# Values of 64-wide heads stationary in column halves, outputs split straight from PSUM, probabilities scaled on GpSimd

## What is computed

```python
s = jnp.einsum('bqhd,bkhd->bhqk', q_i, k_i).astype(jnp.float32) + bias[None]
s = jnp.where(valid[None, None, None, :], s, NEG_INF)
p = jax.nn.softmax(s, axis=-1).astype(v.dtype)
return jnp.einsum('bhqk,bkhd->bqhd', p, v_i)
```

## Time and profile before

| | us |
|---|---|
| median of 3 runs | 2388.64 (2388.24 to 2388.89) |
| the profiled execution | 2387.63 |
| its span, first to last instruction | 2385.8 |
| PE busy | 2359.8 |
| DVE, ACT, POOL busy | 1457.3, 1213.2, 139.7 |

### The profile page before, as it was taken

One profiled execution on the slowest core, in us unless ns is written; L12 is line 12 of the kernel. 1 busy time (PEld: TensorE's weight loads), 2 busy tenths in 40 slices (PEclk: granted clock), 3 DMA queues, 4 the chain that ended last, 5 costly groups with the idle time before them and its releaser, 6 DMA issues.

```text
span 2385.8 us, 30340 instructions
## 1 busy us (share of the span) xinstructions
PE 2359.8 (99%) x11608; PEld 1975.4 (83%) x11608; DVE 1457.3 (61%) x2224; ACT 1213.2 (51%) x1838; POOL 139.7 (6%) x133
## 2 busy tenths in 40 slices
PE   8999999999999999999999999999999999999999
PEld 7888878878888888788888888888888889888887
DVE  5556775565557855565487656654755577556554
ACT  5555544435556444354466654544544476555443
POOL 1430000014210000000000000000000000000000
PEclk9999999999999999999999999999999999999999
DMA  8545456545455565555554445655555544445553
GB/s 299 167 152 198 163 202 234 185 160 170 159 190 168 179 221 184 169 186 193 170 191 145 159 142 168 208 184 180 203 190 190 176 160 142 159 155 190 177 194 106
DMA packets 118078, 427.55 MB, mean 179 GB/s; under 512 B 13616, under 2 KB 14384, under 8 KB 116912
## 3 DMA queue, kind: packets, MB, share of 16 engines
q1 hardware_dynamic: 117792, 425.56, 52.9%
q10 hardware_dynamic: 144, 0.07, 0.0%
HBM read 424.52 MB, written 1.05 MB: 178 GB/s over the span
## 4 chain that ended last, share of the span: by engine, by line
PE 95%; DVE 3%; ACT 1%; DMA 1%; issue 0%; POOL 0%; DVEq 0%; ACTq 0%
PE bank L1878 28%; PE bank L1880 27%; PE bank L1879 27%; PE bank L1935 5%; PE bank L1866 1%; PE bank L1867 1%; PE bank L1868 1%; DVE wl L1446 0%; PE bank L1980 0%; DMA raw<-in_weights 0%; PE bank L1953 0%; PE bank L2003 0%; ACT wh L1235 0%; DVE x L1611 0%; DVE xl L1458 0%
## 5 line engine op out<-in xcount | busy, mean ns | idle before, releaser
L1235 ACT ACTIVATE wh<-raw 128x1024 fp32r<-128x1024 f32 (+1 forms) x778 | 814.9, 1052 | 916.0 <-PE bank L1880 876.7
L1446 DVE TENSOR_TENSOR wl<-raw,wh 128x1024 fp32r<-128x1024 f32 (+1 forms) x778 | 939.3, 1222 | 462.1 <-ACT wh L1235 457.9
L1878 PE MATMUL bank<-wh,xh 128*128 128x512 f32 (+1 forms) x2176 | 867.2, 399 | 9.3 <-DVE xl L1458 6.1
L1880 PE MATMUL bank<-wh,xl 128*128 128x512 f32 (+1 forms) x2176 | 848.6, 390 | 0.0
L1879 PE MATMUL bank<-wl,xh 128*128 128x512 f32 (+1 forms) x2176 | 846.7, 389 | 0.0
L1878 PEld LDWEIGHTS bank<-wh,xh 128*128 128x128 f32 x2176 | 410.4, 189 | 91.8 <-issue 12.5
L1880 PEld LDWEIGHTS bank<-wh,xl 128*128 128x128 f32 x2176 | 410.0, 188 | 86.3
L1879 PEld LDWEIGHTS bank<-wl,xh 128*128 128x128 f32 x2176 | 411.0, 189 | 78.1
L1878 PE MATMUL bank<-wh,act_h 128*128 128x512 f32 x528 | 207.1, 392 | 0.0
L1880 PE MATMUL bank<-wh,act_l 128*128 128x512 f32 x528 | 205.6, 389 | 0.0
L1879 PE MATMUL bank<-wl,act_h 128*128 128x512 f32 x528 | 205.5, 389 | 0.0
(11 more groups left out here) (339 smaller groups left out, 2233.9 us busy)
## 6 DMA issues: line engine op xcount, KB each, us to landing
raw<-in_weights SPq DMA_DIRECT2D x760, 512.0 KB, 3.3
raw<-in_weights SPq DMA_DIRECT2D x16, 384.0 KB, 3.0
ln<-in_ln SPq DMA_DIRECT2D x4, 1024.0 KB, 6.4
bias<-in_bias SPq DMA_DIRECT2D x2, 1024.0 KB, 10.5
b_merge<-in_b_merge SPq DMA_DIRECT2D x2, 1024.0 KB, 5.6
gain<-in_gain_ffn SPq DMA_DIRECT2D x4, 512.0 KB, 3.8
decay<-in_decay SPq DMA_DIRECT2D x2, 768.0 KB, 12.0
x<-in_x SPq DMA_DIRECT2D x2, 512.0 KB, 5.1
```

The source lines that it names most:

```text
L1235: act.activation(wh[:, u % NH, 0:used(u)], raw[:, u % NR, 0:used(u)], ACT.Copy).then_inc(hi_done, 1)
L1446: dve.tensor_tensor(wl[:, u % NR, 0:used(u)], raw[:, u % NR, 0:used(u)], wh[:, u % NH, 0:used(u)].bitcast(F32), ALU.subtract).then_inc(lo_ ...
L1878: pe.matmul(out, h, w_h, start=st.first and i == 0, stop=False)
L1880: last = pe.matmul(out, lo, w_h, start=False, stop=st.last and i == st.nk - 1)
```

## The change

Values and probabilities change sides. Of each pair of heads the values (64 columns wide) are stationary, head h in column half 0 to 63 of the array and head h+1 in 64 to 127, and the transposed probabilities are the moving side: 256 columns for the first key tile, 128 for the second. `OB` then holds the outputs already transposed, features on the partitions, and a new step `o_split`, once every four heads, splits it straight into the high and low parts: ACT copies, DVE subtracts. `ca_out`, `aa_out` and the transposes of the outputs go. Since queries now lie along the columns, the probabilities are scaled before their transpose: a new step `even` takes the reciprocals of the sums on DVE, and POOL multiplies `Pn` by them, four multiplies a pair; `probs_T` waits for POOL (`evened`) in place of ACT (`soft`). A function `heads` lays out both attentions: in round j the evening of pair j-1, the scores of pair j, the values of pair j-2, then the two transposes of pair j-1. The exponential of the sink term is taken for every pair. `m_spread` moves ahead of the attention, and buffers of `ob` and `ha` move.

The strings of the weave are new, for all side work. In block 1 eight dense units (those of `rq` and `rk`) now stand ahead of the first turn of `cq`, where there was one, and seven in place of one behind the last turn. In dense units behind the start of the weave, the first side steps of block 1 then stand so: turns of `cq` at 8, of `ck` at 10, the scores of pair 0 at 11 and of pair 1 at 12 (with the evening of pair 0 ahead of it), transposes of head 0 at 13 and head 1 at 14, scores of pair 2, values of pair 0 and transpose of head 2 at 15. In the two blocks together the number of units is unchanged.

```diff
-UNITS_AMONG_1 = "10122203110102121111010010110201111101011111111111223210111011101011421"
-UNITS_AMONG_2 = "00030102010110200201000111002010210020020100011300000100100411111101000101021021011"
-LAG = 2
+UNITS_AMONG_1 = "802011011100011000011101113201120100110103021301223110011010102011207"
+UNITS_AMONG_2 = "0001020110011121010210100200101111001110050010111011110011101101000101020040102"
...
+def heads(p, of, n, scores, kept):
+
+
+    turn, done = {}, {}
+    for j in range(n + 2):
+        if 1 <= j <= n:
+            i = 2 * j - 2
+            done[i], done[i + 1] = p.count("even"), p.count("even")
+            p.add("even", h=i, of=of, soft=soft, m=p.count("shares"))
+        if j < n:
+            soft = scores(2 * j)[1]
+        if j >= 2:
+            i = 2 * j - 4
+            if i % 4 == 0:
+                o = p.next_o()
+            p.add(of + "_pv", h=i, o=o, t=turn[i + 1], kept=kept)
+            if i % 4 == 2:
+                p.add("o_split", h=i, o=o, dst="ob" if of == "ca" else "ha", n=p.count("hi"), m=p.count("o_ready_0"))
+        if 1 <= j <= n:
+            for h in (2 * j - 2, 2 * j - 1):
+                turn[h] = p.next_t()
+                p.add("probs_T", h=h, t=turn[h], of=of, n=done[h], slot=h % 4)
+    return o
+
...
-    for i in range(CH + LAG + 1):
-        if i < CH and i % 2 == 0:
-            sm[i], sm[i + 1] = scores("ca_s", i, t_c)
-        if LAG <= i < CH + LAG:
-            h = i - LAG
-            tt[h] = p.next_t()
-            p.add("probs_T", h=h, t=tt[h], of="ca", n=sm[h], slot=h % 4)
-        if i > LAG:
-            h = i - LAG - 1
-            if h % 4 == 0:
-                o = p.next_o()
-            p.add("ca_pv", h=h, o=o, t=tt[h], kept=q["cv"])
-            if h % 4 == 3:
-                p.add("ca_out", h=h, o=o)
-    t_b = split_rows("cq", "ob", 4, after_o=o + 1)
+    ob_o = heads(p, "ca", CH // 2, lambda i: scores("ca_s", i, t_c), q["cv"])
...
-        merge(1, j, "w_branch_b", "ob", 4, t_b, j)
+        merge(1, j, "w_branch_b", "ob", 4, None, j, ob_o + 1)
...
     p.add("m_log2")
+    p.add("m_spread", t=t_a)
     tt, sm = {}, {}
-    for i in range(AH + LAG + 1):
-        if i < AH and i % 2 == 0:
-            p.add("aa_s", h=i, s=p.next_s(), t=p.next_t(), after_t=t_a, mx=p.count("maxed"))
-            sm[i], sm[i + 1] = p.count("soft"), p.count("soft")
-        if LAG <= i < AH + LAG:
-            h = i - LAG
-            tt[h] = p.next_t()
-            p.add("probs_T", h=h, t=tt[h], of="aa", n=sm[h], slot=h % 4)
-        if i > LAG:
-            h = i - LAG - 1
-            if h % 4 == 0:
-                q["o"] = p.next_o()
-            p.add("aa_pv", h=h, o=q["o"], t=tt[h], kept=q["akv"])
-            if h % 4 == 3:
-                p.add("aa_out", h=h, o=q["o"], soft=sm[h])
-    t_a2 = split_rows("aqk", "ha", KT, after_o=q["o"] + 1)
-    p.add("m_spread", t=t_a2)
+    q["o"] = heads(p, "aa", AH // 2, scores, q["akv"])
...
-        end = buf("ob_h", [P, 4, S], F32R, at=c0 + 4096)
-        buf("ob_l", [P, 4, S], F32R, at=end)
+        end = buf("ob_l", [P, 4, S], F32R, at=c0)
+        buf("ob_h", [P, 4, S], F32R, at=end)
         end = buf("oc_h", [P, 4, S], F32R, at=e0 + 4096)
...
-        end = buf("ha_h", [P, KT, S], F32R, at=z0)
-        buf("ha_l", [P, KT, S], F32R, at=end)
+        buf("ha", [P, KT, 2, S], F32R, at=z0 - 2048)
...
                                 last.then_inc(roped, 1)
                             else:
                                 link(last)
+                    elif st.kind == "even":
+                        pool.wait_ge(shares, st.m)
+                        for i in range(2):
+                            for r in (1, 0):
+                                part = b["Pn"][:, (st.h + i) % 4, 0:256] if r else b["Pn"][:, (st.h + i) % 4, 256:384]
+                                at = 2 * (st.h % 8) + 2 * r + i
+                                last = pool.tensor_scalar(part, part, rc[:, at:at + 1], None, ALU.mult)
+                            last.then_inc(evened, 1)
                     elif st.kind == "m_spread":
...
                                        scale=st.scale).then_inc(t_hi, 1)
+                    elif k == "o_split":
+                        act.wait_ge(o_ready_0, st.m)
+                        act.wait_ge(o_ready, st.o + 1)
+                        act.activation(split_of[st.dst][0][:, st.h // 2 - 1:st.h // 2 + 1, :],
+                                       OB[:, :].rearrange("p (k n) -> p k n", k=2), ACT.Copy).then_inc(t_hi, 1)
...
                                                       accum_out=sm2[:, at:at + 1])
-                            if n % 4 == 3:
-                                last = act.activation(of4(es, n // 4), of4(es, n // 4), ACT.Exp)
+                            if n % 2:
+                                last = act.activation(of2(es, st.h), of2(es, st.h), ACT.Exp)
...
-                    elif k == "ca_out":
-                        dve.wait_ge(o_ready, st.o + 1)
-                        g = st.h // 4
-                        for r in range(R):
-                            link(dve.reciprocal(rc[:, 4 * r:4 * r + 4], sm[:, r * CH + 4 * g:r * CH + 4 * g + 4]))
-                        for r in range(R):
-                            dst = b["cq"][:, r, 256 * g:256 * g + 256].rearrange("p (h n) -> p h n", h=4)
-                            last = dve.tensor_tensor(dst, OB[:, 256 * r:256 * r + 256].rearrange("p (h n) -> p h n", h=4),
-                                                     rc[:, 4 * r:4 * r + 4].unsqueeze(2).broadcast_to([P, 4, CDH]),
-                                                     ALU.mult)
-                        last.then_inc(o_done, 1)
+                    elif k == "even":
+                        dve.wait_ge(soft, st.soft)
+                        n = st.h
+                        r3 = of2(rc, n).rearrange("p (r h) -> p r h", r=R)
+                        if st.of == "ca":
+                            ins = dve.reciprocal(r3, sm.rearrange("p (r h) -> p r h", r=R)[:, :, n:n + 2])
+                        else:
+                            link(dve.tensor_tensor(r3, sm2.rearrange("p (r h) -> p r h", r=R)[:, :, n:n + 2],
+                                                   of2(es, n).rearrange("p (r h) -> p r h", r=R), ALU.add))
+                            ins = dve.reciprocal(r3, r3)
+                        ins.then_inc(shares, 1)
+                    elif k == "o_split":
+                        dve.wait_ge(t_hi, st.n)
+                        h, lo = [w[:, st.h // 2 - 1:st.h // 2 + 1, :] for w in split_of[st.dst]]
+                        dve.tensor_tensor(lo, OB[:, :].rearrange("p (k n) -> p k n", k=2), h.bitcast(F32), ALU.subtract)\
+                           .then_inc(o_done, 1)
...
-                        if n % 4 == 2:
-                            link(ins)
-                            g = n - 2
-                            ins = dve.tensor_tensor(of4(es, g // 4).rearrange("p (r h) -> p r h", r=R),
-                                                    nmx2.rearrange("p (r h) -> p r h", r=R)[:, :, g:g + 4],
-                                                    b["vec2"][:, 128 + g:132 + g].unsqueeze(1).broadcast_to([P, R, 4]), ALU.add)
+                        link(ins)
+                        ins = dve.tensor_tensor(of2(es, n).rearrange("p (r h) -> p r h", r=R), nm,
+                                                b["vec2"][:, 128 + n:130 + n].unsqueeze(1).broadcast_to([P, R, 2]), ALU.add)
                         ins.then_inc(maxed, 1)
-                    elif k == "aa_out":
-                        dve.wait_ge(o_ready, st.o + 1)
-                        g = st.h - 3
-                        r3 = rc[:, 0:8].rearrange("p (r h) -> p r h", r=R)
-                        dve.wait_ge(soft, st.soft)
-                        link(dve.tensor_tensor(r3, sm2.rearrange("p (r h) -> p r h", r=R)[:, :, g:g + 4],
-                                               of4(es, g // 4).rearrange("p (r h) -> p r h", r=R), ALU.add))
-                        link(dve.reciprocal(rc[:, 0:8], rc[:, 0:8]))
-                        for r in range(R):
-                            dst = b["aqk"][:, r, ADH * g:ADH * g + 256].rearrange("p (h n) -> p h n", h=4)
-                            last = dve.tensor_tensor(dst, OB[:, 256 * r:256 * r + 256].rearrange("p (h n) -> p h n", h=4),
-                                                     rc[:, 4 * r:4 * r + 4].unsqueeze(2).broadcast_to([P, 4, ADH]), ALU.mult)
-                        last.then_inc(o_done, 1)
                     elif k in ("merge2", "ple"):
                         if st.early:
                             dve.wait_ge(first_done, st.early)
@@ -1843,6 +1851,8 @@
                                 pe.wait_ge(d_done[2 * st.pair + r], st.nth)
                         if st.after_t is not None:
                             turned(st.after_t)
+                        if st.after_o:
+                            pe.wait_ge(o_done, st.after_o)
```

(46 more changed lines are left out.)

46 lines of the change are left out of this document (23 added, 23 removed).

## The result

| | before | after |
|---|---|---|
| median, us | 2388.44 (2386.96 to 2388.89, 4 runs) | 2373.81 (2373.66 to 2374.47, 4 runs) |
| ratio, 95% interval | | 0.994 (0.9925 to 0.9956) |
| span of the profiled execution | 2385.8 | 2371.6 |

The kernel after is faster by 14.6 us, 13.4 had been forecast. The two spans differ by 14.2.

A forecast was written before the change was run, and what follows sets the result against it. PE was taken as the bound, so its time counts one for one: -11.8 - 5.3 + 3.4 + 0.3 = -13.4 us, median 2388.64 to 2375.2. Own range 2368 to 2383; 8-in-10 range 2367 to 2389.

The forecast's parts named there:

- Part 1: PE, probabilities times values: a pair falls from 1.34 to 0.85 us as column halves overlap; 11.8 us gained (9.1 to 14.2).
- Rival A: PE value matmuls: column halves don't overlap, a pair costs 1.39 us; 2388.2 us, no change; chance 0.16.
- Part 2: PE, turning of the outputs: 48 transposes of cq and aqk go, 0.11 us each; 5.3 us gained.
- Part 3: DVE and ACT: output splits, reciprocals and extra exponentials stay covered behind dense units; no price.
- Part 4: PE transposes waiting for POOL's evening: block 1 loses 1.7 us in each layer, 3.4 (0 to 6.2); block 2 0.6.
- Part 5: Moves, with `m_spread` before the attention: PE's 0.3 us wait at the turns of `mo` goes.
- Rival B: POOL between exponentials and `probs_T`: evening takes 7.0 us a pair and becomes the bound, 31 us of waits, 2406 us; chance 0.12.

The follow-up runs named there:

- the doubled kernel: Kernel after with each pair's four value matmuls done twice, 2389.04 us; likewise kernel before with each 64-wide head's three done twice, 2419.48 us.
- same_half: Kernel after with both heads of a pair in the same column half, one head's matmuls behind the other's; 2389.28 us.
- late_t0: Kernel after with one dense unit of block 1 moved from behind the attention's last step to ahead of the first transpose; 2386.34 us.
- t0_beside: Kernel after with one dense unit of block 1 moved from between the first two transposes to ahead of them; 2372.14 us.
- pool_twice: Kernel after with each POOL multiply of the evening preceded by a multiply by 1.0 over the same part; 2394.95 us.

## Why the prediction was right, point by point

**The bound.** PE is the bound before and after, and the only wait that came with the change is one that the text had named. Start to start on PE was the right measure.

**Part 1, values.** The new pair was put at 0.85 between 0.75 and 0.96, and is 0.81 in the lines above, 0.80 over all 24. The old pair was put at 1.34, and over the whole trace its 48 heads take 0.58 to 0.71, 0.64 on average, so 1.28 a pair. Start to start, waits left out, all value steps take 30.6 us before and 19.2 after: 11.4 gained, where 11.8 was forecast. The two errors nearly cancel. The parts of the new pair held: 0.65 for both halves together (the doubled kernel), and 0.16 for the change of form where 0.1 had been taken from the scores. The doubled kernels give the gain by another way: 31.1 for 48 heads, against 15.2 plus 24 x 0.16 for 24 pairs, 12.1 us. The Trainium skill's TensorEngine Tiling page (Performance Considerations) has the swap with 2x column tiling for 64 free columns. The trace agrees for the stream, two heads in 0.65 us where one took 0.65. The sum by it, 0.65 a pair and 16.6 us, is 5.2 too good: 3.8 by the change of form (24 x 0.16) and the rest by the old pair's price. The page's Key Properties warn of a drain at such a change; that the 0.16 is this drain no run here shows by itself. Rival A (no overlap) falls: same_half is what it describes, and it takes 15.5 us more. That kernel also shows rival A under-priced: a pair takes 1.44 where it had 1.39.

**Part 2, transposes.** 5.3 predicted. Doubling them costs 0.11 each in the trace and 4.4 us in the medians. Start to start the transposes of `cq` and `aqk` take 9.5 us before and 4.6 after, so 4.9 came.

**Part 3, no price.** No wait of PE for `o_split` or for the reciprocals is in the list of after, and the one new wait for a late `lo`, 0.5 us, also comes without the change. But the cover is thinner than "a unit or more" sounds. In late_t0 a reciprocal moved behind other work of DVE, and what it cost was 7.6 and 6.4 us in the two layers, not a late `lo`: the chain to the transposes broke first.

**Part 4, the wait.** The place was right (T of head 0, block 1, both layers), and the cause (the ropes ahead in POOL's queue). The size was not: 1.7 each was forecast and 1.0 came. The term that was mis-sized most is the ropes' length: 26.3 us were taken over from the kernel before, and in the kernel after they run from 58.09 to 83.45, 25.4. They start 26.5 us ahead of PE's arrival at the transpose (84.61), as the plan had it, but 8 of their 24 instructions take over 1 us where 9 did, and the long ones differ; the text had put this to zero at the bottom of its range. POOL's first head then takes 2.0 us (83.42 to 85.46), more than the 1.7 put down for it, so it is ready 0.85 us behind PE's arrival. Its multiply was over-priced when free: the uncollided pair takes 2.99 us (4 pieces, at 99.46) where the line between 5461 and 566 ns gave 4.2; over all pairs the means are 1217 and 735 ns, close to the 1.2 and 0.9 taken. For block 2 0.6 had been put down, and no wait came there.

**Part 5.** The 0.3 us of `mo` went, as forecast.

**The sum with measured terms.** In the two traces, start to start: values -11.4, turning of the outputs -4.9, all other work of PE +0.1. The waits grew by 1.9: 1.8 for POOL, 0.5 for the late `lo` and 0.2 for the first load of `ident`, less the 0.3 of `mo` and 0.3 on other lines. In all -14.3, against -14.2 in the spans and -14.6 in the medians, so nothing of size is left over. One profiled execution differs from the next by about a microsecond (the span of t0_beside is 3.1 us below that of the kernel after, its median 1.7), so the tenths are not to be leaned on. The forecast of -13.4 took values and turning 0.4 too large each, the wait 1.6 and block 2 0.6 too dear, and had none of the 0.5 that came beside them: that it lies within a microsecond of the result is in part these errors offsetting each other.

**Rival B.** It was wrong for this kernel and right as a mechanism: with 7 us a pair on POOL the whole change loses, 2394.95 against 2388.2. Its price had been 31 us of waits, and 14 of waits and 5 of clock came, since pairs with more slack stay hidden. Its condition failed at the duration: a pair is 3.0 to 3.7 us in block 1 and 3.5 to 4.8 in block 2, 3.9 on average, and 28 of the 96 multiplies are over 1.0 us (256 columns) or 0.7 (128), not all of them.

**A better kernel.** Two variants remove the remaining waits, 2372.14 and 2371.65 against 2373.81. Both are below the kernel before by well over the noise; against the kernel after, 1.7 and 2.2 us are near the 1.8 that the theory asks for but under 0.1% of the time, so that step is carried by the vanished waits in the trace and not by the medians alone.

## What to carry to other kernels

When heads are 64 wide, put values stationary in the two column halves and issue both: at these sizes (256 and 128 moving columns) a head's matmuls were then free beside its neighbour's, and the price was 0.16 us per group, so keep them in groups. Before a unit of cover is moved, look at what else stands between the producer and its queue on every engine: one unit, right on paper, put a 0.18 us reciprocal behind 2.9 us of gates and ate twelve of the fifteen us. And a wait of PE can cost more than itself: behind 4.9 us the clock came down and took 2.5 and 1.3 us more, behind 0.8 and 0.9 us nothing.

## What the runs showed of the hardware that I had not expected

- Column halves overlap whatever the order in the queue: four matmuls A, A, B, B take 0.81 us as do A, B, A, B; in one half they take 1.44.
- The stalls of PE of 2.3 us (pool_twice, first evening) and 4.9 us (late_t0) lie in windows with a granted clock of 0.89, and the next are at 0.94 and 0.76; around the 0.84 us stall of the kernel after it is 1.00. Behind 4.9 us the slow unit cost 2.5 us more in one layer and 1.3 in the other, so the same wait has no fixed price. The kernel before has such a stretch of its own: its wait of 4.2 us for `x`, which ends at 515.20, lies in a window (510 to 520) with a granted clock of 0.67.
- POOL's multiply by a column of scalars takes 0.92 us on 256 columns and 0.60 on 128 when it runs freely; its tensor by tensor product on 256 columns takes 0.74.
